# Three VectorE operations that find the experts' order, moved from ahead of the plan's arithmetic to behind its hot matrices

## The chip, the core and the metric

The kernel runs on one core of one Trainium2 chip. The metric is the device time of one execution in microseconds; lower is better. One execution was also recorded by the hardware profiler, and all rows below are from that one.

The engines are TensorE (PE in the rows, with PEld for its weight loads), VectorE (DVE), ScalarE (ACT), GpSimd (POOL) and SyncE (SP), which here only starts transfers. A "q" behind an engine's name (SPq, POOLq) marks its instruction queue where it issues a transfer.

## What is computed

One step of an encoder layer over 1024 prompt tokens and 64 sample tokens, width 1024, all in float32: a mixer with two recurrent head groups, then a mixture of experts, then a final norm. The change touches the mixture of experts alone:

```python
def hier_moe(h, lp):
    lg = t @ lp["w_router_group"] + lp["b_router_group"]        # 4 groups, the best one is taken
    le = ...                                                    # the 4 experts of that group
    top_v, top_i = lax.top_k(jax.nn.softmax(le, axis=-1), 2)    # the best two of them
    ...
    for e in range(16):
        hid = jax.nn.silu(t @ w_expert_gate[e]) * (t @ w_expert_up[e])
        out = out + comb[:, e:e + 1] * (hid @ w_expert_down[e])
```

## The kernel before

The kernel is a row of blocks; the one that matters is `experts_block`. It doesn't multiply every token with every expert. It first makes a **plan**: how many tokens each expert has, the order of the experts by that number (the fullest first), and which token goes to which place of which tile. Then it runs through the 16 experts in that order, two buffers in turn (`wg`, `wu`, `wd` hold gate, up and down weights of two experts, 2048 KB each and expert).

The plan is a chain on VectorE. The helper `then` (every operation of the chain waits for the one before) is used nearly throughout. In the order of the program:

- `total`, the counts of each expert, comes out of PSUM (L2725). L2727 to the reduction behind L2728 give `place`, each expert's rank by count, and L2731 gives the 16 by 16 matrix `loads`, which says which expert stands at which rank (it lies in the buffer `ended`, so the rows call it `moe_ended`).
- L2732 to L2734 are the three operations of this change. From row 0 of `loads` they make `order`, 16 integers, the number of the expert at each rank: a product into `found` (which lies in the buffer `sil`), a reduction into `order_f`, and a cast into `order`, which raises the semaphore `order_made`.
- L2736 to L2763 give each choice of each token its tile and its position in the tile.
- L2769 and L2772 make `at_tile`, L2775 (three operations) makes `at_pos`. These are the plan's hot matrices. TensorE multiplies them in 18 products (36 records), L2466, as each third of `at_pos` comes; the sum is the list of tokens of every tile.
- L2779 casts that list into `plan_token` and raises `plan_made`.

Who waits for what:

- **SyncE** waits for `order_made` at the head of its program. Then for each rank p it reads `order[p]` and starts the three transfers of this expert's weights (L2348, L2350, L2352). Ahead of those of rank 1 it waits until both first gathers have landed (`x0_loaded`, `x1_loaded`); from rank 2 on each buffer is waited for (`gate_done` and so on).
- **GpSimd** waits for `plan_made` and then gathers the tokens of a tile out of HBM by `plan_token`, an indirect DMA (L2416) into `xg`, of which there are two. The first two (a tile of the fullest experts' tails, and the main tile of rank 0) are issued back to back, the others as the buffers come free.
- **TensorE** waits for `plan_made`, runs 11 products of the identity that nothing reads (`keep_running`, 22 records of L176), and then turns the two gathered tiles, each as it lands (`turn_tile`, L2472). ScalarE and VectorE copy the turned tiles into `xT`, and the product of gate with `xT` (L2487) starts, if the gate weights are there.

The transfers of all queues share the core's 16 DMA engines.

Of the kernel before, what the change touches and what calls it, by code (L numbers as in the profile page):

```python
# [8 lines left out]
ALU = mybir.AluOpType  # L9
# [16 lines left out]
NE, NG, EG = 16, 4, 4  # L26
# [2199 lines left out]
def experts_block(nc, a, d, c, psum, final_rows):  # L2226
# [5 lines left out]
    with nc.cleanup_on_exit(), ExitStack() as ctx:  # L2232
        sems = {}

        def sg(name):
            if name not in sems:
                sems[name] = nc.alloc_semaphore(name="moe_" + name)
            return sems[name]

        def sb(name, shape, dt=F32):  # L2240
            return ctx.enter_context(nc.sbuf_tensor("moe_" + name, shape, dt))
# [18 lines left out]
        count = sb("count", [P, P])  # L2260
# [9 lines left out]
        order_f, order = sb("order_f", [1, NE]), sb("order", [1, NE], I32)  # L2270
# [4 lines left out]
        loads = ended[:, 0:NE, :]  # L2275
# [14 lines left out]
        found = sil[:, :, :].rearrange("p a s -> p (a s)")[:, 0:2 * NE * NE].rearrange("p (i e n) -> p i e n", i=2, e=NE)  # L2290
# [375 lines left out]
        def _(dve):  # L2666
            done = [0]

            def then(op):

                done[0] += 1
                op.then_inc(sg("route_step"), 1)
                dve.wait_ge(sg("route_step"), done[0])
# [5 lines left out]
            V = nc.vector  # L2679
            def reduce(out, in_, op):  # L2680
                return V.tensor_reduce(out=out, in_=in_, axis=AX_X, op=op)
# [47 lines left out]
            then(reduce(place[:, :], loads, ALU.add))  # L2729

            then(V.tensor_tensor(loads, place[:, :].unsqueeze(2).to_broadcast(ALL2), count[:, 0:NE].unsqueeze(1).to_broadcast(ALL2), ALU.is_equal))  # L2731
            then(V.tensor_tensor(found[0:1, 0, :, :], loads[0:1].rearrange("p e n -> p n e"), count[0:1, 0:NE].unsqueeze(1).to_broadcast([1, NE, NE]), ALU.mult))  # L2732
            then(reduce(order_f[0:1, :], found[0:1, 0, :, :], ALU.add))
            V.tensor_copy(order[0:1, :], order_f[0:1, :]).then_inc(sg("order_made"), 1)  # L2734

            then(V.tensor_tensor(found[:, :, :, :], loads.unsqueeze(1).to_broadcast([P, 2, NE, NE]), c["by_place"][:, :, :].unsqueeze(2).to_broadcast([P, 2, NE, NE]), ALU.mult))  # L2736
            then(reduce(taken_place[:, :, :], found[:, :, :, :], ALU.add))
            then(V.tensor_tensor(start[:, :], total, size, ALU.subtract))
# [26 lines left out]
            def choices(v):  # L2765
                return v.rearrange("p n i -> p (n i)").unsqueeze(2)
# [7 lines left out]
            for n in range(0, NT, 3):  # L2774
                V.tensor_tensor(at_pos[:, n:n + 3, :, :].rearrange("p n i c -> p (n i) c"), count_i[:, :].unsqueeze(1).to_broadcast([P, 6, P]),  # L2775
                                choices(pos_i[:, n:n + 3, :]).to_broadcast([P, 6, P]), ALU.is_equal).then_inc(sg("pos_hot"), 1)

            dve.wait_ge(sg("plan_done"), 1)
            V.tensor_copy(plan_token[:, :], psum[2][:, 0:NTILE]).then_inc(sg("plan_made"), 1)  # L2779
# [239 lines left out]
```

## Time and profile before

| | us |
|---|---|
| median of 3 runs | 1477.74 |
| lowest, highest | 1475.89, 1479.08 |
| the profiled execution, its time | 1477.55 |
| its span in the trace | 1475.8 |
| TensorE busy in the span | 1364.1 (92%) |
| VectorE busy in the span | 460.1 (31%) |
| mean share of the 16 DMA engines by the weights' queue | 45.7% |

Times in the rows are counted from the start of the span. The experts' block begins near 967, the plan's chain at 968, and the product of the first expert at 1005. A timeline row gives start, length, engine, line, operation, what is written from what, and in brackets the idle time ahead of it with what ended it. PEclk is the TensorE clock that was granted, as a share of 2.4 GHz: 1.00 is 2.4 GHz and 0.50 is 1.2 GHz.

### The profile page before, as it was taken

Reading aid. Unit: us, or ns where it says so; the run is one execution under the profiler, and the core shown is the slowest. Engines: PE = TensorE matmul, PEld = TensorE weight load, DVE = VectorE, ACT = ScalarE, POOL = GpSimd, SP = SyncE. Lnnn points to the kernel's source line nnn. Section 1 sums busy time; section 2 is a strip of 40 time slices with the busy share of each in tenths; the row PEclk is TensorE's granted clock in tenths of the full one; section 3 lists DMA queues with packets and bytes.
Section 4 is the critical chain, followed back from the end, with each engine's and each line's share of the span. In section 5 each row is a group of like instructions: output and inputs, shape, how many; then the busy total and the mean of one; then the engine's idle time right before and its main releaser. Section 6 shows DMA issues by size and latency. Waiting matters only on the chain. (4 is left out here: it accounts for less than half of the span.)

```text
span 1475.8 us, 23429 instructions
## 1 busy us (share of the span) xinstructions
PE 1364.1 (92%) x9607; PEld 965.9 (65%) x9607; DVE 460.1 (31%) x811; ACT 357.7 (24%) x715; POOL 230.4 (16%) x522
## 2 busy tenths in 40 slices
PE   5899999999999689999999998939999999999965
PEld 3466666656666486776667666438788787878832
DVE  4245546460020125343544343252000010000018
ACT  6321322320211223342334232101111111111123
POOL 5102111123000103113320330011000000000043
PEclk9899999999999779999999998959999999999988
DMA  9427466453223554433343330159779997898358
GB/s 346 131 88 254 151 228 211 142 194 96 73 74 107 149 183 93 123 98 84 89 113 98 93 73 1 42 180 330 275 257 388 397 386 277 326 333 323 143 201 299
DMA packets 194373, 274.85 MB, mean 186 GB/s; under 512 B 44168, under 2 KB 114886, under 8 KB 194264
## 3 DMA queue, kind: packets, MB, share of 16 engines
q1 hardware_dynamic: 170296, 223.13, 45.7%
q0 software_dynamic: 12688, 39.55, 7.1%
q10 hardware_dynamic: 11280, 10.62, 2.3%
q8 instruction: 80, 1.31, 0.4%
q14 instruction: 29, 0.24, 0.1%
HBM read 215.85 MB, written 57.41 MB: 185 GB/s over the span
## 5 line engine op out<-in xcount | busy, mean ns | idle before, releaser
L2487 PEld LDWEIGHTS banks<-moe_xT,moe_wg 128*128 128x128 f32 x1024 | 131.3, 191 | 8.9 <-issue 7.8
L2487 PE MATMUL banks<-moe_xT,moe_wg 128*128 128x128 f32 (+4 forms) x1024 | 135.3, 290 | 0.8 <-ACT moe_xT L2591 0.8
L2487 PE MATMUL banks<-moe_xT,moe_wu 128*128 128x128 f32 (+4 forms) x1024 | 134.3, 289 | 0.0
L2487 PEld LDWEIGHTS banks<-moe_xT,moe_wu 128*128 128x128 f32 x1024 | 131.2, 191 | 0.0
L1489 PE MATMUL banks<-mixer_w_out,mixer_yT 128*128 128x512 f32 x256 | 121.7, 619 | 0.0
L730 PE MATMUL banks<-xT,w_v 128*128 128x352 f32 (+1 forms) x384 | 118.7, 469 | 1.9 <-ACT sig_w L894 1.9
L730 PE MATMUL banks<-xT,w_r 128*128 128x352 f32 (+1 forms) x384 | 118.6, 469 | 0.0
L730 PE MATMUL banks<-xT,w_k 128*128 128x352 f32 (+1 forms) x384 | 118.4, 468 | 0.0
L2516 PE MATMUL banks<-moe_wd,moe_hid 128*128 128x512 f32 x256 | 112.5, 592 | 0.0
L730 PEld LDWEIGHTS banks<-xT,w_v 128*128 128x128 f32 x384 | 72.5, 190 | 45.7 <-issue 2.9
L730 PEld LDWEIGHTS banks<-xT,w_k 128*128 128x128 f32 x384 | 72.9, 190 | 43.9
L730 PEld LDWEIGHTS banks<-xT,w_r 128*128 128x128 f32 x384 | 72.7, 190 | 43.9 <-issue 0.6
L2828 DVE TENSOR_TENSOR moe_hid<-moe_sil,banks 128x256 f32<-128x256 f32 (+4 forms) x16 | 7.4, 460 | 242.6 <-PE banks L2487 242.6
L2516 PEld LDWEIGHTS banks<-moe_wd,moe_hid 128*128 128x128 f32 x256 | 47.4, 190 | 53.6 <-issue 53.6
L1489 PEld LDWEIGHTS banks<-mixer_w_out,mixer_yT 128*128 128x128 f32 x256 | 47.3, 194 | 51.8 <-issue 48.1
L1833 POOL TENSOR_TENSOR mixer_LTm<-mixer_LT,level 128x256 f32<-128x256 f32 (+1 forms) x36 | 25.4, 735 | 253.0 <-ACT mixer_LTo L1912 223.2
L2416 POOL DMA_INDIRECT moe_xg<-moe_input,moe_plan_token x19 | 18.2, 959 | 241.6 <-PE banks L2472 216.0
L674 POOL DMA_DIRECT2D mod_rows<-mod x48 | 24.7, 521 | 184.7 <-DVE mod L1048 184.6
L2833 DVE TENSOR_TENSOR moe_hid<-moe_sil,banks 128x256 f32<-128x256 f32 (+4 forms) x16 | 7.4, 460 | 121.3 <-PE banks L2487 121.3
L2947 PE MATMUL banks<-final_y,final_diag 128*128 128x512 f32 (+1 forms) x72 | 35.3, 642 | 9.0 <-DMA final_y<-expert_rows,slots 6.6
L2623 ACT COPY moe_yrow<-banks 128x512 f32<-128x512 f32 x32 | 18.7, 586 | 100.7 <-PE banks L2516 100.7
L1440 PE MATMUL banks<-feats 64*128 64x128 f32 (+1 forms) x320 | 25.5, 309 | 15.3 <-DMA feats<-feature_major 9.1
(505 smaller groups left out, 1962.8 us busy)
## 6 DMA issues: line engine op xcount, KB each, us to landing
moe_wg<-w_expert_gate SPq DMA_DIRECT2D x16, 2048.0 KB, 9.6
moe_wu<-w_expert_up SPq DMA_DIRECT2D x16, 2048.0 KB, 13.6
moe_wd<-w_expert_down SPq DMA_DIRECT2D x16, 2048.0 KB, 11.4
feats<-w_ada SPq DMA_DIRECT2D x8, 2048.0 KB, 7.8
wada<-w_ada SPq DMA_DIRECT2D x4, 2048.0 KB, 24.6
feats<-w_ada_final SPq DMA_DIRECT2D x4, 2048.0 KB, 8.2
expert_rows<-moe_yrow ACTq DMA_DIRECT2D x16, 512.0 KB, 6.2
expert_rows<-moe_xTo SPq DMA_DIRECT2D x16, 512.0 KB, 14.4
```

Source lines behind the costliest of these rows:

```text
L674: pool.dma_start(d["mod"][:, bass.ds(at + P * r, P)], mod[32 * r:32 * r + 2, :]).then_inc(sg("ada_stored"), 16)
L730: mm = pe.matmul(out_of(dst, i), w[:, q, :], hT[:, q, lo:hi], start=q == 0, stop=q == KT - 1)
L1440: mm = pe.matmul(banks_[g][0:m, i * P:i * P + m], lhs[q, j, 0:m], rhs[q, j, 0:m], start=True, stop=True)
L1489: mm = pe.matmul(psum[4 + half if late else 4 - 2 * half][0:m, :], yT[:, q, 0:m], w_out[:, q, 512 * half:512 * half + 512], start=q == 0, ...
L1833: nc.gpsimd.tensor_tensor(LTm[0:m, k - 4, g, :, :], LT[0:m, g, :, :], over4(c["level"][0:m, k - 4, :]), ALU.mult).then_inc(sg(f"LTm{g}_mad ...
L2416: pool.indirect_dma_start(out=xg[:, i % 2, :], out_offset=None, in_=d["h2"], in_offset=bass.IndirectOffsetOnAxis(ap=plan_token[:, col:col ...
L2487: mm = pe.matmul(bank[:, i * n:(i + 1) * n], wt[:, p % 2, q, (t0 + i) * P:(t0 + i + 1) * P], xT[:, p % 2, q, 0:n], start=q == 0, stop=q == ...
L2516: mm = pe.matmul(psum[5 + h][:, :], hid[:, q, 0:S_MAIN], wd[:, u, q, 512 * h:512 * h + 512], start=q == 0, stop=q == DE // P - 1)
L2623: nc.scalar.copy(yrow[:, u, 512 * h:512 * h + 512], psum[5 + h][:, :]).then_inc(sg("y_read"), 1)
L2828: V.tensor_tensor(hid[:, 0:2, 0:n], sil[:, 0:2, 0:n], halves(psum[1], p), ALU.mult).then_inc(sg("hid_made"), 1)
L2833: V.tensor_tensor(hid[:, 2:4, 0:n], sil[:, 2:4, 0:n], halves(psum[7], p), ALU.mult).then_inc(sg("hid_made"), 1)
L2947: mm = pe.matmul(pair(n)[0:m, 512 * h:512 * h + 512], diag[0:m, n, i, 0:m], y[0:m, n, 512 * h:512 * h + 512], start=i == 0, stop=i == 1)
```

## The change

The three operations L2732 to L2734 are taken from where they stood, directly behind `loads`, and put behind the three operations that make `at_pos`, ahead of the wait for TensorE's list. Nothing is added or removed, and no other engine's program differs.

```diff
             then(V.tensor_tensor(loads, place[:, :].unsqueeze(2).to_broadcast(ALL2), ..., ALU.is_equal))
-            then(V.tensor_tensor(found[0:1, 0, :, :], loads[0:1].rearrange("p e n -> p n e"), count[0:1, 0:NE]..., ALU.mult))
-            then(reduce(order_f[0:1, :], found[0:1, 0, :, :], ALU.add))
-            V.tensor_copy(order[0:1, :], order_f[0:1, :]).then_inc(sg("order_made"), 1)
-
             then(V.tensor_tensor(found[:, :, :, :], loads.unsqueeze(1)..., c["by_place"]..., ALU.mult))
...
             for n in range(0, NT, 3):
                 V.tensor_tensor(at_pos[:, n:n + 3, :, :]..., ALU.is_equal).then_inc(sg("pos_hot"), 1)
+
+            then(V.tensor_tensor(found[0:1, 0, :, :], loads[0:1].rearrange("p e n -> p n e"), count[0:1, 0:NE]..., ALU.mult))
+            then(reduce(order_f[0:1, :], found[0:1, 0, :, :], ALU.add))
+            V.tensor_copy(order[0:1, :], order_f[0:1, :]).then_inc(sg("order_made"), 1)
 
             dve.wait_ge(sg("plan_done"), 1)
             V.tensor_copy(plan_token[:, :], psum[2][:, 0:NTILE]).then_inc(sg("plan_made"), 1)
```

VectorE's program where the ranks of the experts are done, before:

```order
L2681 TENSOR_REDUCE moe_place<-moe_ended 128x16
L2731 TENSOR_TENSOR moe_ended<-moe_place,moe_count 128x256
L2732 TENSOR_TENSOR moe_sil<-moe_ended,moe_count 1x256
L2681 TENSOR_REDUCE moe_order_f<-moe_sil 1x16
L2734 CAST moe_order<-moe_order_f 1x16
L2736 TENSOR_TENSOR moe_sil<-moe_ended,by_place 128x512
L2681 TENSOR_REDUCE moe_taken_place<-moe_sil 128x32
```

The same place of the changed kernel:

```order
L2681 TENSOR_REDUCE moe_place<-moe_ended 128x16
L2731 TENSOR_TENSOR moe_ended<-moe_place,moe_count 128x256
L2732 TENSOR_TENSOR moe_sil<-moe_ended,by_place 128x512
L2681 TENSOR_REDUCE moe_taken_place<-moe_sil 128x32
L2734 TENSOR_TENSOR moe_start<-moe_total_s,moe_taken_place 128x16
```

The plan's arithmetic follows the ranks at once. VectorE's program where the hot matrices are made, in the changed kernel:

```order
L2765 TENSOR_TENSOR moe_at_tile<-moe_count_i,moe_tile_i 128x630
L2768 TENSOR_TENSOR moe_at_tile<-moe_at_tile,moe_token 128x630
L2771 TENSOR_TENSOR moe_xT<-moe_count_i,moe_pos_i 128x768 x3
L2774 TENSOR_TENSOR moe_sil<-moe_ended,moe_count 1x256
L2681 TENSOR_REDUCE moe_order_f<-moe_sil 1x16
L2776 CAST moe_order<-moe_order_f 1x16
L2779 CAST moe_plan_token<-banks 128x35
```

The three operations now stand between the last third of `at_pos` (`moe_xT` in the rows, whose buffer it uses) and the cast of the plan.

## Rows read from the trace of the kernel before

**Rows 1.** Windows view of the experts' stretch; columns in its first row

```profile
core 0: us, PE busy (x) PEld busy (x) DVE busy (x) ACT busy (x) POOL busy (x), PEclk, DMA share, GB/s
1005.00:1411.80 406.80, 406.79 (x2680) 329.14 (x2680) 28.73 (x51) 46.04 (x90) 18.25 (x24) 1.00 0.83 308
```

**Rows 2.** Timeline from the plan's products to the first expert's product

```profile
988.29 7.86 PE L2466 MATMUL banks<-moe_at_tile,moe_xT 128*128 128x35 f32 x36 [12.95 <-DVE moe_xT L2775]
...
996.19 0.19 DVE L2779 CAST moe_plan_token<-banks 128x35 int32<-128x35 f32 x1 [6.31 <-PE banks L2466]
...
996.44 4.81 PE L176 MATMUL banks<-ident 128*128 128x128 f32 x22 [0.29 <-DVE moe_plan_token L2779]
...
996.68 1.12 POOL L2416 DMA_INDIRECT moe_xg<-moe_input,moe_plan_token  x1 [24.42 <-DVE moe_plan_token L2779]
...
998.10 0.96 POOL L2416 DMA_INDIRECT moe_xg<-moe_input,moe_plan_token  x1 [0.30 <-issue]
...
1001.11 1.09 PE L2472 MATMUL banks<-ident,moe_xg 128*128 128x128 f32 x8
...
1003.09 1.09 PE L2472 MATMUL banks<-ident,moe_xg 128*128 128x128 f32 x8 [0.89 <-DMA moe_xg<-moe_input,moe_plan_token]
...
1005.01 5.44 PE L2487 MATMUL banks<-moe_xT,moe_wg 128*128 128x192 f32 x32 [0.83 <-ACT moe_xT L2591]
```

**Rows 3.** Timeline of VectorE, the operations that move and their neighbours

```profile
977.08 0.57 DVE L2732 TENSOR_TENSOR moe_sil<-moe_ended,moe_count 1x256 f32<-1x256 f32 x1
...
978.21 0.67 DVE L2736 TENSOR_TENSOR moe_sil<-moe_ended,by_place 128x512 f32<-128x512 f32 x1
...
987.19 2.69 DVE L2775 TENSOR_TENSOR moe_xT<-moe_count_i,moe_pos_i 128x768 f32<-128x768 int32 x3
```

**Rows 4.** Timeline of SyncE's queue: first gate load of ranks 0 and 1

```profile
979.30 0.42 SPq L2348 DMA_DIRECT2D moe_wg<-w_expert_gate  x1
...
1003.86 0.38 SPq L2348 DMA_DIRECT2D moe_wg<-w_expert_gate  x1
```

**Rows 5.** DMA view, gathers issued at 996.68 and 998.10; last column us to landing

```profile
moe_xg<-moe_input,moe_plan_token POOLq DMA_INDIRECT x1, 4.4
...
moe_xg<-moe_input,moe_plan_token POOLq DMA_INDIRECT x1, 4.9
```

**Rows 6.** DMA view, issues at 1003.85 to 1003.86, then the gather at 1005.12

```profile
moe_wg<-w_expert_gate SPq DMA_DIRECT2D x1, 2048.0 KB, 12.5
moe_xg<-moe_input,moe_plan_token POOLq DMA_INDIRECT x1, 9.6
...
moe_xg<-moe_input,moe_plan_token POOLq DMA_INDIRECT x1, 10.4
```

**Rows 7.** Tile view of moe_xg, all 19 gathers

```profile
DMA to landing us min/median/max: 4.2/7.7/10.4
```

**Rows 8.** DMA view, rank 0's gate, up and down loads, issued 979.30, 979.83, 980.44

```profile
moe_wg<-w_expert_gate SPq DMA_DIRECT2D x1, 2048.0 KB, 9.5
...
moe_wu<-w_expert_up SPq DMA_DIRECT2D x1, 2048.0 KB, 14.4
...
moe_wd<-w_expert_down SPq DMA_DIRECT2D x1, 2048.0 KB, 18.8
```

**Rows 9.** Windows view, DMA share and GB/s last, columns as in Rows 1

```profile
997.00:998.00 1.00, 1.00 (x7) 1.00 (x6) 0.72 (x5) 0.23 (x1) 0.79 (x1) 0.50 0.33 131
...
1010.00:1037.00 27.00, 27.00 (x139) 20.66 (x137) 1.80 (x3) 2.74 (x5) 0.96 (x1) 1.00 1.04 395
...
1046.00:1053.00 7.00, 7.00 (x51) 6.99 (x50) 1.21 (x2) 0.78 (x2) 1.46 (x2) 1.00 0.27 74
```

**Rows 10.** Windows view around two changes of the granted clock, columns as in Rows 1

```profile
946.98:949.00 2.02, 0.00 (x1) 0.02 (x1) 1.92 (x6) 0.89 (x2) 0.00 (x0) 1.00 0.00 0
...
949.70:953.00 3.30, 3.30 (x10) 1.20 (x8) 1.78 (x3) 1.42 (x3) 0.00 (x0) 0.50 0.03 6
953.00:955.00 2.00, 2.00 (x10) 0.69 (x8) 1.67 (x2) 0.23 (x2) 0.00 (x0) 0.98 0.92 314
996.40:1000.80 4.40, 4.36 (x20) 4.36 (x21) 3.68 (x19) 0.47 (x2) 2.07 (x2) 0.50 0.70 228
1000.90:1005.00 4.10, 2.39 (x19) 1.89 (x19) 2.58 (x7) 1.78 (x3) 1.57 (x2) 1.00 0.33 109
```

**Rows 11.** Timeline of TensorE: rank 1's first product

```profile
1037.31 5.04 PE L2487 MATMUL banks<-moe_xT,moe_wg 128*128 128x176 f32 x32
```

More of the change, by code:

```diff
@@ L2731, in _ @@
             then(V.tensor_tensor(loads, place[:, :].unsqueeze(2).to_broadcast(ALL2), count[:, 0:NE].unsqueeze(1).to_broadcast(ALL2), ALU.is_equal))
-            then(V.tensor_tensor(found[0:1, 0, :, :], loads[0:1].rearrange("p e n -> p n e"), count[0:1, 0:NE].unsqueeze(1).to_broadcast([1, NE, NE]), ALU.mult))
-            then(reduce(order_f[0:1, :], found[0:1, 0, :, :], ALU.add))
-            V.tensor_copy(order[0:1, :], order_f[0:1, :]).then_inc(sg("order_made"), 1)
             then(V.tensor_tensor(found[:, :, :, :], loads.unsqueeze(1).to_broadcast([P, 2, NE, NE]), c["by_place"][:, :, :].unsqueeze(2).to_broadcast([P, 2, NE, NE]), ALU.mult))
@@ L2776, in _ @@
                                 choices(pos_i[:, n:n + 3, :]).to_broadcast([P, 6, P]), ALU.is_equal).then_inc(sg("pos_hot"), 1)
+            then(V.tensor_tensor(found[0:1, 0, :, :], loads[0:1].rearrange("p e n -> p n e"), count[0:1, 0:NE].unsqueeze(1).to_broadcast([1, NE, NE]), ALU.mult))
+            then(reduce(order_f[0:1, :], found[0:1, 0, :, :], ALU.add))
+            V.tensor_copy(order[0:1, :], order_f[0:1, :]).then_inc(sg("order_made"), 1)
             dve.wait_ge(sg("plan_done"), 1)
```

## The prediction

> **What bounds the kernel now.** I read the windows first. From 1005.00 to 1411.80 TensorE is busy in 406.79 of 406.80 us, at a clock of 1.00 [rows 1]. So this stretch is as long as its products; whatever moves its start moves the end of the kernel by as much, unless a later wait appears in it. The question is what sets 1005.01, the start of the first gate product.
>
> The timeline answers it backwards [rows 2]. The product follows the copy of the second turned tile; that tile is turned at 1003.09, when TensorE had idled 0.89 us for the gather of `moe_xg`. The gather was issued at 998.10, behind the first one at 996.68, which waited for the cast of the plan at 996.19. The cast waited for TensorE's 36 records from 988.29 on, and those for VectorE's chain. So the path is: VectorE's chain, plan products, cast, two gathers, turn, product. The weights are not on it: rank 0's gate is issued at 979.30 [rows 4] and lands 9.5 us later, at 988.8; up lands at 979.83 + 14.4 = 994.2 and down at 980.44 + 18.8 = 999.2 [rows 8]. They are there 16 us before the product needs gate. The change spends this slack, and takes something off the chain.
>
> **Step 1, what leaves the chain.** The three operations hold VectorE from 977.08 to 978.21, 1.13 us [rows 3]. All behind them up to the third part of `at_pos` comes 1.13 us earlier. TensorE starts the plan's products at 988.29 - 1.13 = 987.16. They are paced by TensorE itself (7.86 us for 36), and VectorE's 2.69 us for three thirds stay ahead of it, so the cast also comes 1.13 us earlier, at 995.06. The moved operations now run from 987.19 + 2.69 - 1.13 = 988.75 to about 989.88, while VectorE would idle 6.31 us for TensorE [rows 2]: 5 us of cover, cost nothing. If that cover were gone they would cost their 1.13 us again. **Gathers are issued at 995.55 and 996.97: -1.13 us.**
>
> **Step 2, what the weights lose.** Before, `order` was ready at 978.21 at the latest and the first load stood at 979.30, 1.09 us later. Now it is ready at 989.88, so gate is issued at about 990.97, 11.67 us later than before. All three transfers of rank 0 shift with it. Queued behind this wait on SyncE there is only the rest of its own list; rank 1's loads wait for the gathers anyway.
> Is gate in time? Alone it took 9.5 us, which gives 1000.5. Rank 1's gate, which was issued within 0.01 us of a gather, took 12.5 us [rows 6], which gives 1003.5. Both are before 1005.01. Up, by 14.4 us behind 991.5, lands at 1005.9; with the 3 us more of the gate row it is 1009. It is needed one gate product later, at 1010.3 before and later now. Down, by 18.8 + 3, lands at 1013.9, needed from 1026.8 on. **The weights themselves: 0**, with 1.5 us to spare for gate.
>
> **Step 3, what the gathers meet.** This is the step on which the sum turns. Before, the weights' stream had ended when the first gathers moved: from 997 to 998 the DMA engines were busy 0.33 at 131 GB/s [rows 9], and the two gathers landed in 4.4 and 4.9 us [rows 5]. After, 6 MB of weights, issued from 991 on, take until about 990.97 + 19.9 = 1010.9, and both gathers, at 995.55 and 996.97, fall in the middle. What does a gather take then? Over all 19 the median is 7.7 us [rows 7], most of those issued while weights were moving. The nearest pair is the next one: issued at 1003.85 and 1005.12, just as a whole expert's weights were, 1.27 us apart where the first two are 1.42 apart. They took 9.6 and 10.4 us [rows 6]. I take the pair, since a lone gather doesn't share with another. The second tile then lands at 996.97 + 10.4 = 1007.4 where it landed at 998.10 + 4.9 = 1003.0: **+4.4 us**. By the median it would be 1004.7, +1.7 us; undisturbed, 1001.9, -1.1 us.
>
> The Trainium skill, page "DMA: Bandwidth & Descriptors", section "Queues, rings and completion order", says that each engine goes round its queues by whole packets of about 9 to 17 descriptors, so a gather of 8 rows for each engine would wait for little more than one packet of weights. At 395 GB/s over 16 engines, 17 descriptors of 2 KB are an estimate of 1.4 us, and the sum would be -1.1 + 1.4 = +0.3 us instead of +4.4. The landing rows under load don't bear that out: they say 9.6 and 10.4 against 4.4 and 4.9, which is 5 us and not 1.4.
>
> **Step 4, TensorE's clock.** The plan's products run at 0.50, and so does `keep_running` until 1000.8; from 1000.9 on the clock is 1.00 and stays so through the two turns, where TensorE is busy in 2.39 of 4.10 us [rows 10]. After the change `keep_running` ends at 1001.25 - 1.13 = 1000.1, and the first tile lands at 995.55 + 9.6 = 1005.2. TensorE is then idle for 5 us. An idle time of 2.02 us (946.98 to 949.00, with little work ahead of it) was followed by 0.50 from 949.7 to 953.0 [rows 10]. So I expect 1.2 GHz for the turns and the start of the product. The second turn's 8 records take 1.7 us instead of 1.09 (22 of L176 take 4.81 at 0.50 for nearly all of it, 0.22 each): +0.6. The clock came back 4.4 us after dense work began at 996.44 [rows 10], and about 4 us after 949.01. The turn begins at 1007.4 and the product at about 1010, so the product runs at half rate for about 2 us (counted from the turn) to 5.5 us (counted from the product, with a delay); half of that is lost, 1 to 2.7 us; I take 1.9. **+2.5 us** in all, bounds 0 (the clock stays) and +3.5.
>
> **Step 5, afterwards.** Rank 1's weights are issued when the second tile has landed, at 1003.86 before and about 1008.2 now [rows 4]. They queue behind what is left of rank 0's, so the gate of rank 1 lands by about 1008.2 + 12.5 + 3 = 1024; it is needed at 1037.31 + 6.9 [rows 11]. DMA is full at 395 GB/s until 1037 now and has air from 1046 to 1053 (0.27) [rows 9], into which a backlog of 11.67 us less the idle time before goes. No later wait: 0.
>
> **The sum.** -1.13 + (10.4 - 4.9) + 2.5 = **+6.9 us**. The profiled execution took 1477.55, 0.2 from the median of 1477.74, so 1477.55 + 6.9 = 1484.4.
>
> **Rivals.**
> - **Gathers hurt less** (the median, 7.7 us): +1.7, and the clock still falls, since TensorE idles from 1000.1 to 1003.3: +2.5. 1481.7. For it: the loads' stream has been running for 4.6 us when the first gather is issued, and isn't just beginning as at 1003.85. Against: two gathers overlap.
> - **The clock stays.** TensorE restarts before it falls, or it falls late. +1.7 to +4.4, 1479.3 to 1482.0. For it: the clock held over 0.89 us and 0.83 us. Against: the idle time here is 3 to 5 us.
> - **Not slower** (the other side): the gathers pass the weights nearly undisturbed, as in the page's rule. Then -1.1 to +0.3 us, 1476.4 to 1477.9, no change. It decides at the landing time: below 6.0 us for the second gather (4.9 + 1.13) the change gains, and with the clock falling as well, the loss goes under 3 us below about 6.5. Against it: the pair of rows 6. For it: rank 0's gate is partly through by 995.55.
> - **The weights become the bound.** In the forecast the product starts at about 1010, so gate would be the last to come if it took over 19 us to land (990.97 + 19 = 1010), 6.5 us over the gate row of rows 6. At 20 to 22 us the end is 1 to 3 us behind the sum, 1485.5 to 1487.5. For it: both gathers lie in its time. Against: gate is first in the queue.
>
> **Chances.** Sum as forecast 0.43; less hurt gathers 0.20; clock stays 0.13; not slower 0.14; weights as the bound 0.10. The low end has to reach into the clock case, so it is 1478.6, and the high end, with the clock's 3.5 and a gather of 11 us, 1488.0. A measurement of this kernel tells about 0.2%, 3 us, from no change: slower takes the forecast, the weights, most of the less hurt gathers and half the clock case, 0.74; same has the rest, 0.24; faster 0.02, since the only gain in sight is 1.13 us.
>
> **What would show it.** Step 1: the cast of the plan at about 995.1. Step 2: first gate issue near 991. Step 3: the second gather at 10 us to landing, and TensorE's idle ahead of the turns `<-DMA moe_xg`. Step 4: PEclk 0.50 in the first gate product, which then takes over 7 us instead of 5.44. Step 5: no idle of TensorE from there to the end. The forecast is wrong if the gathers land within 6 us, or if the first gate product waits for `moe_wg`.

## The result, and the profile after

The changed kernel is slower, by little: 1482.89 us against 1476.51, medians of 21 runs each taken in turn. The medians lie 6.4 us apart and the means of the same runs 5.2. The ratio follows the means: it is 1.0035, with a 95% interval of 1.0021 to 1.0049, so the loss is 5.2 us, between 3.1 and 7.2. The forecast was 1484.4, +6.9 us. Single runs of either kernel spread over 13 us, so a trace has to be read from a mark inside it. The mark used below is the start of the experts' block's first product on TensorE (L2457). It stands at 972.79 in the trace of before and at 975.90 in that of the change; those 3.11 us lie ahead of anything that the change touches. The whole span differs by 9.9 us (1475.8 and 1485.7), which is why the span of one trace would mislead here.

Timeline of the changed kernel from the mark to the second gate product (start, length, engine, line, operation, in brackets the idle time and what ended it). It answers [rows 2 to 4].

```profile
975.90 0.82 PE L2457 MATMUL banks<-moe_either,after 128*128 128x144 f32 x2 [7.00 <-DVE moe_either L2707]
...
990.30 7.87 PE L2466 MATMUL banks<-moe_at_tile,moe_xT 128*128 128x35 f32 x36 [11.85 <-DVE moe_xT L2771]
991.81 0.56 DVE L2774 TENSOR_TENSOR moe_sil<-moe_ended,moe_count 1x256 f32<-1x256 f32 x1
992.40 0.41 DVE L2681 TENSOR_REDUCE moe_order_f<-moe_sil 1x16 f32<-1x256 f32 x1
992.85 0.16 DVE L2776 CAST moe_order<-moe_order_f 1x16 int32<-1x16 f32 x1
994.02 0.43 SPq L2348 DMA_DIRECT2D moe_wg<-w_expert_gate  x1
...
998.20 0.19 DVE L2779 CAST moe_plan_token<-banks 128x35 int32<-128x35 f32 x1 [5.20 <-PE banks L2466]
...
998.45 5.06 PE L176 MATMUL banks<-ident 128*128 128x128 f32 x22 [0.29 <-DVE moe_plan_token L2779]
...
998.69 1.11 POOL L2416 DMA_INDIRECT moe_xg<-moe_input,moe_plan_token  x1 [23.32 <-DVE moe_plan_token L2779]
...
1000.11 0.96 POOL L2416 DMA_INDIRECT moe_xg<-moe_input,moe_plan_token  x1 [0.30 <-issue]
...
1006.29 1.09 PE L2472 MATMUL banks<-ident,moe_xg 128*128 128x128 f32 x8 [2.78 <-DMA moe_xg<-moe_input,moe_plan_token]
...
1008.35 1.97 PE L2472 MATMUL banks<-ident,moe_xg 128*128 128x128 f32 x8 [0.97 <-DMA moe_xg<-moe_input,moe_plan_token]
...
1011.15 6.90 PE L2487 MATMUL banks<-moe_xT,moe_wg 128*128 128x192 f32 x32 [0.83 <-issue]
...
1017.88 5.36 PE L2487 MATMUL banks<-moe_xT,moe_wu 128*128 128x192 f32 x32
```

Counted from the mark, the plan's products start at 14.40 instead of 15.50: the 1.1 us are gained. The three moved operations follow `at_pos` while TensorE is at the plan, and VectorE still idles 5.20 us behind them, so they cost nothing there. But TensorE now waits 2.78 us for the first gather. The second turn is at 32.45 instead of 30.30, the gate product at 35.25 instead of 32.22, and that product lasts 6.90 us instead of 5.44, so the up product is at 41.98 instead of 37.50. From the DMA view of the changed kernel, the two gathers, issued at 998.69 and 1000.11, and rank 0's gate, up and down (last column us to landing), to be held against [rows 5, 8]:

```profile
moe_xg<-moe_input,moe_plan_token POOLq DMA_INDIRECT x1, 7.6
...
moe_xg<-moe_input,moe_plan_token POOLq DMA_INDIRECT x1, 8.2
...
moe_wg<-w_expert_gate SPq DMA_DIRECT2D x1, 2048.0 KB, 9.4
...
moe_wu<-w_expert_up SPq DMA_DIRECT2D x1, 2048.0 KB, 16.8
...
moe_wd<-w_expert_down SPq DMA_DIRECT2D x1, 2048.0 KB, 23.8
```

And the windows view of the changed kernel (columns as in rows 1; PEclk, the granted clock, is the last but two):

```profile
1003.51:1006.28 2.77, 0.00 (x1) 0.00 (x0) 0.64 (x4) 0.00 (x0) 0.00 (x0) 0.93 1.03 398
...
1007.00:1011.00 4.00, 2.35 (x12) 1.71 (x10) 1.33 (x2) 2.05 (x3) 1.98 (x3) 0.54 1.05 398
1011.20:1013.80 2.60, 2.60 (x8) 2.60 (x9) 0.00 (x0) 0.19 (x1) 0.84 (x2) 0.50 1.02 410
...
1014.20:1017.70 3.50, 3.50 (x23) 3.50 (x22) 0.00 (x0) 0.00 (x0) 0.00 (x0) 1.00 1.02 400
```

The same view in steps of 0.4 us, where the clock rises and where it falls:

```profile
1003.20:1003.60 0.40, 0.31 (x2) 0.01 (x1) 0.40 (x1) 0.00 (x0) 0.00 (x0) 0.50 1.11 415
...
1004.00:1004.40 0.40, 0.00 (x0) 0.00 (x0) 0.18 (x2) 0.00 (x0) 0.00 (x0) 1.00 0.97 379
...
1006.80:1007.20 0.40, 0.40 (x6) 0.35 (x4) 0.00 (x0) 0.21 (x1) 0.00 (x0) 1.00 0.98 379
...
1007.60:1008.00 0.40, 0.00 (x0) 0.00 (x0) 0.40 (x1) 0.00 (x0) 0.00 (x0) 0.50 1.03 384
```

While TensorE waits for the first gather, the DMA engines are full (1.03, 398 GB/s), where in the kernel before the stream had ended by then [rows 9]. The granted clock is still 0.50 (1.2 GHz) when TensorE falls idle at 1003.51, is 1.00 from 1004.0 on and through the first turn, and is back at 0.50 for the second turn and the first part of the gate product; from 1014.2 on it is 1.00.

Three terms, then, make the 4.48 us to the up product: -1.10 for the shorter chain, +3.25 for the second gather's turn, and +2.33 for the clock (0.88 on the turn, 1.45 on the product). The trace has 1.09 us more at rank 5:

```profile
1167.95 4.61 PE L2487 MATMUL banks<-moe_xT,moe_wu 128*128 128x160 f32 x32 [1.09 <-DMA moe_wu<-w_expert_up]
```

and 1.1 us more in TensorE's first wait for the final block's gathers (7.7 against 6.6). Whether those two belong to the change is one of the questions below.

### The profile page after: what moved, and what is told of

Its sections match the earlier page's. It is cut to its first block and busy times, and to the rows that moved or that the text cites. A ratio compares the mean times of both kernels' runs of the same rounds, so it can differ in the third digit from the quotient of the medians.

```text
span 1485.7 us, 23429 instructions
## 1 busy us (share of the span) xinstructions
PE 1371.2 (92%) x9607; PEld 972.6 (65%) x9607; DVE 459.9 (31%) x811; ACT 358.0 (24%) x715; POOL 229.5 (15%) x522
```

## The experiments

The theory: the late loads put the weights' stream beside the two first gathers, which delays them, and TensorE's longer idle time costs it the clock. Its rivals: the new place of the operations on VectorE costs something itself; the clock is no term of its own; a gather waits for what is queued and not for what moves; the loads must be early because the products need the weights.

A table first. All distances are us from the mark of the same trace; the landing is that of the two first gathers. A blank is a number that the trace didn't give (no landing, or two turns in one row) or a kernel with a single time. A ratio is to runs of the kernel before in the same group of runs; its own median was 1476.51, 1475.49, 1478.57 and 1480.81 us in the four groups, so times of different groups can't be compared directly.

| kernel | first gate issue | gathers to landing | second turn | gate product | up product | ratio to before |
|---|---|---|---|---|---|---|
| before | 6.51 | 4.4, 4.9 | 30.30 | 32.22 | 37.50 | |
| before_again | 6.51 | 4.4, 5.0 | 30.35 | 32.27 | 37.54 | |
| the change | 18.12 | 7.6, 8.2 | 32.45 | 35.25 | 41.98 | 1.0035 |
| late_loads | 18.17 | 7.7, 8.3 | | 36.48 | 43.68 | 1.0039 |
| after_keep22 | 18.12 | 7.5, 8.2 | 32.43 | 34.35 | 39.63 | 1.0018 |
| hold_all | 30.33 | 4.2, 5.0 | 29.29 | 42.30 | 48.96 | |
| gate_first | 18.12 | 6.1, 5.9 | 30.33 | 32.95 | 42.87 | |
| after_hold_down | 18.13 | | 32.43 | 35.23 | 42.04 | 1.0022 |
| order_pool | 8.55 | 6.9, 6.7 | 31.29 | 33.89 | 41.34 | 1.0010 |
| order_pool_hold_down | 8.55 | 4.4, 5.1 | 29.49 | 31.41 | 36.68 | 0.9958 |
| order_pool_hold_down2 | 8.54 | | 29.36 | 31.29 | 36.56 | 0.9995 |
| before_hold_down | 6.51 | | 30.51 | 32.44 | 37.71 | 1.0004 |

**Late loads alone, `late_loads`.** VectorE's program is that of before; only SyncE waits longer.

```diff
             sp.wait_ge(sg("order_made"), 1)
+            sp.wait_ge(sg("pos_hot"), 3)
             for p in range(NE):
```

> The kernel before, with VectorE's program as it was; SyncE alone waits, ahead of its first load, for the third part of at_pos besides the order. So the loads come about 11 us later and the chain keeps its 1.13 us. I measure from the start of the experts' block's first product on TensorE: 32.22 us to the first gate product and 37.50 to the first up product before, 35.25 and 41.98 in the changed kernel. If the late loads are the cause, the gathers land in 7.5 to 9 us instead of 4.4 and 4.9, TensorE's clock falls to 0.50 ahead of the gate product, and the distances are those of the changed kernel plus 1.1: about 36.4 and 43.1, in time 5 to 7 us over the kernel before. If instead the moved operations themselves cost (VectorE's new place, what waits for them), the distances stay at 32.2 and 37.5.

Measured: ratio 1.0039 (1.0020 to 1.0058), gate product at 36.48, up at 43.68. Its timeline (the lines are one further on in this kernel):

```profile
1005.44 4.03 PE L2473 MATMUL banks<-ident,moe_xg 128*128 128x128 f32 x16 [3.79 <-DMA moe_xg<-moe_input,moe_plan_token]
...
1010.30 7.37 PE L2488 MATMUL banks<-moe_xT,moe_wg 128*128 128x192 f32 x32 [0.83 <-DVE moe_xT L2811]
```

TensorE idles 3.79 us for the gather and the gate product takes 7.37 us. The up product comes 1.7 us later than in the change: 1.2 at the gate product, nearly all of it the 1.1 that the chain keeps, and 0.5 of a longer gate product. With nothing moved on VectorE, the whole loss is there. So the loads' lateness carries it, and the moved operations on VectorE are a gain of 1.1 us by the rows; the two times (1.0039 and 1.0035) can't tell that gain.

**A longer run of the identity, `after_keep22`.**

```diff
-            keep_running(pe, psum[6], ident, 11)
+            keep_running(pe, psum[6], ident, 22)
```

> The changed kernel with 22 products of the identity in place of 11 ahead of the turns. TensorE then works until about the first tile's landing. If the fall of the clock is a term of its own (0.9 us on the second turn, 1.5 us on the gate product), the clock stays at 1.00, the gate product takes 5.4 us instead of 6.90, the distance to the first gate product is about 34.4 and to the first up product 39.6 (37.50 before, 41.98 in the changed kernel). If the wait for the gathers is all there is and the clock would have fallen or not regardless, the up product stays at 42. Over the kernel before by 2 to 3.5 us.

Measured, as expected: ratio 1.0018 (1.0001 to 1.0035), up product at 39.63. From its timeline:

```profile
994.47 7.82 PE L176 MATMUL banks<-ident 128*128 128x128 f32 x44 [0.29 <-DVE moe_plan_token L2779]
...
1002.30 1.09 PE L2472 MATMUL banks<-ident,moe_xg 128*128 128x128 f32 x8
...
1004.35 1.09 PE L2472 MATMUL banks<-ident,moe_xg 128*128 128x128 f32 x8 [0.96 <-DMA moe_xg<-moe_input,moe_plan_token]
...
1006.27 5.44 PE L2487 MATMUL banks<-moe_xT,moe_wg 128*128 128x192 f32 x32 [0.83 <-ACT moe_xT L2591]
```

The gathers land as late as in the change (second turn at 32.43 and 32.45), but both turns take 1.09 us and the gate product 5.44. The clock is a term of its own: 41.98 - 39.63 = 2.35 us, which is the 2.33 read from the changed kernel's rows. What is left against before is 39.63 - 37.50 = 2.13 us, -1.10 for the chain and +3.2 for the gathers.

**No stream at all beside the gathers, `hold_all`.** SyncE waits for both gathers' landing ahead of its first load.

```diff
             sp.wait_ge(sg("order_made"), 1)
+            for u in range(2):
+                sp.wait_ge(sg(f"x{u}_loaded"), 16)
             for p in range(NE):
```

> The changed kernel, but SyncE starts no load before both first gathers have landed. If the weights' stream is what slows the gathers, they land in 4.4 and 4.9 us again, and the second turn comes 1.1 us earlier than in the kernel before: 29.2 us from the block's first product. Then the gate product waits for its weights, issued about 1 us behind the landing and 9.5 us long: distance about 40 us to the gate product. If the gathers are slow because of their new time or of VectorE, they still take 7.6 and 8.2.

```profile
moe_xg<-moe_input,moe_plan_token POOLq DMA_INDIRECT x1, 4.2
...
moe_xg<-moe_input,moe_plan_token POOLq DMA_INDIRECT x1, 5.0
```

Those are its gathers in the DMA view, and this is its gate product in the timeline:

```profile
1016.45 6.82 PE L2489 MATMUL banks<-moe_xT,moe_wg 128*128 128x192 f32 x32 [11.91 <-DMA moe_wg<-w_expert_gate]
```

Its one time is 1490.44, beside 1475.49 for before. The gathers are as fast as before, at the same early time as in the change, and the second turn is at 29.29, 1.0 us ahead of before. The rival that their new time or VectorE slows them falls. The weights then become the bound, at 11.91 us of idle; gate took 11.8 us to land and not the 9.5 that I had put. The two gathers for the next tiles were issued within 1.4 us of it, as beside the 12.5 us of [rows 6]; that they are the reason isn't tested. So the early place of the loads has two reasons: the product needs gate, and the stream has to be over when the gathers move.

**A third of the stream, `gate_first`.** Rank 0's up and down wait for the gathers, gate doesn't.

```diff
                 w(sp, "up_done", before)
+                if isinstance(before, int) and before < 0:
+                    for v in range(2):
+                        sp.wait_ge(sg(f"x{v}_loaded"), 16)
                 sp.dma_start(wu[:, u], ...)
```

> The changed kernel, but of rank 0's three loads only gate is issued ahead of the gathers' landing, up and down behind it. 2 MB of the stream meet the gathers instead of 6. If a gather is slowed only while weights move beside it, the first lands in 5.5 to 7 us and the second, which begins when gate has nearly landed, in 5 to 6; the gate product comes at 31.5 to 33 us. The up product then waits for its weights, which are issued at about 31 and take 10 to 12: about 42. If the wait grows with what is queued and not with what moves, both stay near 7.6 and 8.2.

Its one time is 1482.32, beside a median of 1475.49 for before. Measured: gathers 6.1 and 5.9 us, gate product at 32.95, up at 42.87 with TensorE idle 2.3 us for `moe_wu`. As expected, with the clock down again: the gate product takes 7.59 us and the up product 7.15.

```profile
1003.67 7.59 PE L2490 MATMUL banks<-moe_xT,moe_wg 128*128 128x192 f32 x32 [0.83 <-issue]
...
1013.59 7.15 PE L2490 MATMUL banks<-moe_xT,moe_wu 128*128 128x192 f32 x32 [2.33 <-DMA moe_wu<-w_expert_up]
```

The gathers lie between those of `hold_all` (4.2 and 5.0) and those of the change (7.6 and 8.2).

**Two thirds of the stream, `after_hold_down`.** The same three lines ahead of `wd` instead of `wu`, in the changed kernel.

> The changed kernel with rank 0's down weights held until both gathers have landed: 4 MB of stream instead of 6, issued about 4 us ahead of the first gather and moving until some 14.5 us behind its issue. If a gather is slowed by what moves while it moves, both gathers lie wholly in the 4 MB and take the same 7.6 and 8.2 us, the gate product stays near 35 and the up product near 42. If it is slowed by how much is queued behind, they land earlier, by a third of the delay: 6.5 and 7, gate product near 34.

```profile
1008.96 1.09 PE L2475 MATMUL banks<-ident,moe_xg 128*128 128x128 f32 x8 [2.78 <-DMA moe_xg<-moe_input,moe_plan_token]
...
1011.00 1.97 PE L2475 MATMUL banks<-ident,moe_xg 128*128 128x128 f32 x8 [0.95 <-DMA moe_xg<-moe_input,moe_plan_token]
```

Waits of 2.78 and 0.95 us, turns of 1.09 and 1.97: the rows of the changed kernel nearly digit for digit, with 2 MB less in the queue. The trace has no landings of its gathers. Holding back the last third, which in the change landed at 1019, nearly 11 us behind the second gather, changes nothing. So what is queued behind doesn't delay a gather, as far as this third goes, and what moves beside it does. The ratio of 1.0022 (1.0005 to 1.0038) is of 10 runs and overlaps that of the change.

**The order on GpSimd, `order_pool`.** From the kernel before; VectorE loses the three operations, GpSimd gets a product, four halving additions and a cast. Not shown in these lines: VectorE signals `loads_made`, and waits for `order_made` far behind the plan, before it writes over the matrix.

```diff
+            pool.wait_ge(sg("loads_made"), 1)
+            G_.tensor_tensor(order_w[:, :, :], loads[0:1]..., count[0:1, 0:NE]..., ALU.mult).then_inc(sg("order_step"), 1)
+            for i, h in enumerate((8, 4, 2, 1)):
+                pool.wait_ge(sg("order_step"), i + 1)
+                G_.tensor_tensor(order_w[:, :, 0:h], order_w[:, :, 0:h], order_w[:, :, h:2 * h], ALU.add).then_inc(sg("order_step"), 1)
+            pool.wait_ge(sg("order_step"), 5)
+            G_.tensor_copy(order[0:1, :], order_w[:, :, 0]).then_inc(sg("order_made"), 1)
             pool.wait_ge(sg("plan_made"), 1)
```

> The kernel before, with the order found on GpSimd, which idles there: a product, four halving additions and a cast behind the matrix of ranks, and nothing of it on VectorE. VectorE's chain is 1.13 us shorter, as in the change, and the loads start early. On GpSimd six small operations of 0.2 to 0.6 us with their waits take 2 to 3.5 us, so the loads start 1 to 2.5 us later than before and the stream ends that much nearer to the gathers, which come 1.1 us earlier. If only the meeting of loads and gathers costs, the distance to the first gate product is 31.1 to 32.5 (32.22 before), to the up product 36.4 to 37.8 (37.50); clock as before; time within 1.5 us of the kernel before, not to be told from no change. If taking the operations off the chain itself harmed, it would be like the changed kernel, 35.25 and 41.98.

Measured: ratio 1.0010 (0.9995 to 1.0025), gate product at 33.89, up at 41.34. That is a miss: I had put 32.5 and 37.8 as the worst. Its timeline:

```profile
1001.16 1.09 PE L2481 MATMUL banks<-ident,moe_xg 128*128 128x128 f32 x8 [2.08 <-DMA moe_xg<-moe_input,moe_plan_token]
1002.58 1.77 PE L2481 MATMUL banks<-ident,moe_xg 128*128 128x128 f32 x8 [0.33 <-ACT moe_xTt L2600]
...
1005.18 7.61 PE L2496 MATMUL banks<-moe_xT,moe_wg 128*128 128x192 f32 x32 [0.83 <-issue]
```

The loads start 2.04 us later than before and the gathers 0.92 us earlier, and those 3 us are enough: the gathers take 6.9 and 6.7 us, TensorE idles 2.08 us, and its clock falls. The gathers' part (second turn 0.99 us later, behind a chain that is 0.92 us ahead, so 1.9) is smaller than the clock's: the second turn takes 1.77 us and the gate product 7.61, and from the second turn to the up product it is 10.05 us instead of 7.20. The time over 12 runs gives +1.5 us, at most 3.7, and the trace 3.84; that would fit with a clock which doesn't fall in every execution, but only one was traced, so this stays open.

**The order on GpSimd with down held, `order_pool_hold_down`.** As above, and rank 0's down waits for the gathers.

> As the run with the order on GpSimd, and rank 0's down weights are issued only when both first gathers have landed. Gate and up, 4 MB, end before the gathers begin. If the meeting is the cause, both gathers land in 4.4 to 4.9 us and the distance to the first gate product is 31.1 (32.22 before), the best that this step can give; down is needed 16 us behind the second gather and lands in 10 to 13. Time 1.1 us under the kernel before at the most, which is within what a measurement can tell.

```profile
1000.42 1.09 PE L2484 MATMUL banks<-ident,moe_xg 128*128 128x128 f32 x8 [0.67 <-DMA moe_xg<-moe_input,moe_plan_token]
...
1002.34 5.44 PE L2499 MATMUL banks<-moe_xT,moe_wg 128*128 128x192 f32 x32 [0.83 <-DVE moe_xT L2820]
```

Gathers 4.4 and 5.1 us, a second turn of 1.09 and a gate product of 5.44 us, so the clock held; gate product at 31.41 (I had put 31.1), up at 36.68: 0.82 us ahead of before. This is what the shorter chain can give, once nothing meets the gathers. The ratio was 0.9958 from six runs, 6 us, which no row explains. So it was timed again, as `order_pool_hold_down2`, with its neighbour `before_hold_down` beside it, in which the order stays on VectorE and only down is held.

> The same kernel as order_pool_hold_down, for its time. Its trace explains 0.8 us (up product 36.68 us behind the block's first product, 37.50 before), its ratio of 0.9958 from six runs would be 6 us. If the trace holds all there is, the ratio now comes out near 0.9995, within 0.2% of no change, and the first ratio was the spread of few runs. If the kernel has something outside this stretch, the ratio is near 0.996 again.

> The kernel before, with the order on VectorE as it was, and rank 0's down weights issued only when both first gathers have landed. In the kernel before the stream ended as the gathers began, so there is next to nothing to clear: gathers 4.3 to 4.9 us, gate product at 32.0 to 32.3 and up product at 37.3 to 37.5 (37.50 before), time within 0.1% of the kernel before. If holding down has an effect of its own elsewhere, it shows here as 4 to 6 us less, as in the first ratio of order_pool_hold_down.

Measured: 0.9995 (0.9980 to 1.0011) for the first and 1.0004 (0.9986 to 1.0022) for the second, with up products at 36.56 and 37.71. The time of `before_hold_down` is as expected; its products, 32.44 and 37.71, are 0.1 and 0.2 us behind the range that I had put, so holding down gives nothing by itself. The second ratio of the kernel with both edits fits its trace; the first, of six runs in another group and on another chip, doesn't, and their intervals (0.9942 to 0.9973 and 0.9980 to 1.0011) don't meet. I take the six runs for low by chance; that isn't shown. The kernel with both edits is ahead of before by 0.8 to 0.9 us in both its traces and by nothing that a time can tell. It is the fastest of the study by its rows; it isn't shown to be so by its time.

**A second trace of the kernel before, `before_again`.**

> The kernel before, unchanged, for a second trace of it. Both theories expect 32.2 and 37.5 us from the block's first product to the gate and up products. It is to tell whether TensorE's wait of 1.09 us for rank 5's up weights in the trace of the change is one that the kernel before has too in some executions (its weights landed 0.6 us ahead of need there), and how far the stretch up to the experts' block varies.

The distances repeat within 0.05 us (32.27, 37.54), while the mark moved from 972.79 to 968.56. And TensorE's waits of this trace in the experts' stretch have a line for `moe_wu`:

```profile
PE banks L2487 <- DMA moe_wu<-w_expert_up: 0.5, 1, 0.5
```

So the kernel before has this wait too, in some executions. It was 0 in the first trace of before, in `late_loads`, `after_keep22` and `gate_first`, 0.5 here, 0.6 in `after_hold_down`, 1.0 in `hold_all` and 1.09 in the change. It comes with kernels whose loads are late and with one whose loads are not, and is missing in three whose loads are late. So its being there isn't shown to be the change's doing; whether late loads make it longer stays open. Rank 5's loads queue behind 26 transfers of zeros and rows on SyncE, and its up weights landed close to their need in other kernels too: 1.6 us ahead in `late_loads`, 0.6 in the first trace of before, 0.1 in `gate_first` and in `order_pool`. The other question was the first wait in the final block: it was 6.8 us here, 6.6 to 7.1 in the experiments, 6.6 in the first trace of before and 7.7 in the change. So it moves by half a microsecond from trace to trace, and one reading of 7.7 isn't shown to be the change's either.

## Why the prediction was right

The time lies in the range, the sign is right, and the size is three quarters of the forecast (5.2 of 6.9 us).

- **The bound** was read rightly: plan, gathers, turn, gate product, with the experts' stretch as long as its products. The up product's delay of 4.48 us is found again at the last down product (432.06 and 437.90 from the mark, 5.84 later; the other 1.36 all come at rank 5, 1.09 of them the wait).
- **Step 1**, -1.13: measured -1.10, and the moved operations are covered.
- **Step 2**, loads 11.67 us later: measured 18.12 - 6.51 = 11.61. Gate took 9.4 us, not up to 12.5; no product waited for rank 0's weights.
- **Step 3** is the term that was mis-sized. I put the second gather at 10.4 us, by the pair issued at 1003.85 and 1005.12 [rows 6]; it took 8.2, so +3.3 instead of +5.5. The pair I chose were gathers three and four, issued together with rank 1's loads; the two of the change were issued 4.7 and 6.1 us behind rank 0's first load. That difference repeats: gathers three and four took 9.7 and 10.5 in `before_again`, 8.9 and 9.3 in the change and 8.4 and 9.1 in `late_loads`, and the first two, 4.7 to 7.1 us behind the first load, 7.5 to 8.3 in all three kernels that have the whole stream there. It isn't only that a stream begins: in the change rank 0's down weights were still moving, with the DMA engines full (1.05), when gathers three and four were issued. Why these two are slower isn't shown. The median of all gathers, 7.7, which I gave to a rival, was the better row.
- **The page's rule**, Trainium skill, "DMA: Bandwidth & Descriptors", section "Queues, rings and completion order", says that an engine goes round its queues by whole packets. My estimate from it was 1.4 us of delay; the gathers lost 3.2 and 3.3. That they get in between agrees with the trace: they landed at 1006.3 and 1008.3, ahead of up (1011.4) and down (1019.0), which had been issued before them. The size was not what I made of it.
- **Step 4**, the clock: +2.5 forecast, +2.33 measured, and confirmed by `after_keep22`. The way there was wrong in part, and there is some luck in the number: I had put 5 us of idle time and 1.2 GHz for both turns. TensorE idled 2.77 us, since the first gather came in 7.6 us and not 9.6; the clock, which had risen up to half a microsecond after `keep_running` ended, was 1.00 for the first turn and fell at its end. The gate product took 6.90 us, just under the "over 7" that I had named as the sign.
- **Step 5**, no later wait: the sign that I had named, no idle time of TensorE to the end, didn't come, since TensorE waited 1.09 us at rank 5. Whether the change makes that wait is open, since `before_again` has it too, if shorter. What I missed is that the kernel before stands 0.6 us from a wait at rank 5: up was issued there at 1132.92, landed 25.6 us later, at 1158.5, and its product began at 1159.10. I had read the backlog from 1037 to 1053 and no further.
- Of the rivals, "gathers hurt less" (1481.7) came nearest with its landing times, "not slower" fell, and the weights as the bound were seen only in `hold_all`, where I made them so.
- **The high end** of the range doesn't follow from its terms: 1477.55 - 1.13 + (11 - 4.9) + 3.5 is 1486.0, and not 1488.0. The measured 1482.89 lies in the range either way.

## What to carry to other kernels

A transfer with slack to its own consumer may still have none to spare: look at what else will move on the DMA engines at its new time, and price a small transfer on the critical path by rows in which it ran beside such a stream (here 4.9 us alone, 8.2 in the midst of it, 10.4 in the pair that I had taken). Then add what the longer idle time does to TensorE's clock, which made two fifths of the gross loss here, and more of it in `order_pool`. And where runs spread by 13 us, measure a change of 1 to 5 us from a mark inside the trace, not by the span.

## What was not expected of the hardware

- The two first gathers take 4.2 to 5.1 us where the stream is over as they begin to move (eight readings, in two traces of before, in `hold_all` and in `order_pool_hold_down`), 5.9 to 6.9 us where it ends beside them (`gate_first`, `order_pool`) and 7.5 to 8.3 in the midst of it. The last third of it, queued behind, made no difference to the turns (`after_hold_down`).
- The cost of a fall of the clock can be larger than that of the delay that brings it about: in `order_pool` a second turn 0.99 us later came with 2.85 us more from there to the up product. In the change it was the other way, 2.33 for the clock and 3.25 for the gather.
- The order on GpSimd, six operations on one partition with 256 elements and less, took 3.2 us, from 975.63 to 978.82 in the trace of `order_pool`, against 1.13 us for three on VectorE.
